# A layer norm's gain and offset: folded into the group's output, or applied to the whole block on GpSimd

## The reference

```
v = layernorm(gelu(v_raw), ln_w, ln_b)         # over the 1024 channels of a token
vc = v.reshape(b, 4, 128, 8, 128)              # chunk, token, group, channel
mixed = einsum('gts,bnsgc->bntgc', w_s, vc) + b_s[group, token]
y_b = gelu(u_raw) * mixed * silu(g_raw)
```

## Time and profile before

| | |
|---|---|
| time of three runs | 1870.9 us median (1867.78 to 1877.06) |
| the profiled execution | 1870.9 us, its span 1869.0 us |
| mean granted TensorE clock | 0.949 |
| busy: TensorE, VectorE, ScalarE, GpSimd | 90%, 43%, 33%, 28% |
| head phase, gate phase | about 49 to 490 us, about 490 to 670 us |

### The profile page before, as it was taken

How to read it: one execution, slowest core, us unless ns; L and a number is a source line. 1 busy time by engine, 2 the same in 40 slices (tenths; PEclk the granted TensorE clock), 3 DMA queues, 4 the chain that set the end, 5 groups by cost and what they waited for, 6 DMA issues and landing times.

```text
span 1869.0 us, 22809 instructions
## 1 busy us (share of the span) xinstructions
PE 1680.4 (90%) x9242; PEld 1301.9 (70%) x9242; DVE 801.9 (43%) x1246; ACT 625.8 (33%) x1008; POOL 531.5 (28%) x279
## 2 busy tenths in 40 slices
PE   4999989899899789998968998999996889999996
PEld 2888878799687667776737897555683665555564
DVE  2237377464674520111156611666413445444422
ACT  3421222212323222223232122666413223555632
POOL 2331222212122343334324222332423321010230
PEclk8999999899999889999989999999997889999998
DMA  4231322212323425443301221000010120000101
GB/s 136 91 125 36 100 68 67 74 38 67 90 81 88 125 76 171 135 135 112 102 23 46 68 75 45 18 18 18 23 57 26 30 65 20 15 18 24 46 23 46
DMA packets 128674, 122.46 MB, mean 66 GB/s; under 512 B 11237, under 2 KB 125041, under 8 KB 128593
## 3 DMA queue, kind: packets, MB, share of 16 engines
q1 hardware_dynamic: 128592, 121.33, 20.8%
HBM read 116.87 MB, written 2.10 MB: 64 GB/s over the span
## 4 chain that ended last, share of the span: by engine, by line
PE 64%; DVE 13%; issue 12%; POOL 7%; ACT 3%; DMA 1%; SPq 0%; DVEq 0%; POOLq 0%; ACTq 0%
PE ps L1771 6%; PE ps L1772 5%; PE ps L1773 5%; PE ps L1817 5%; POOL w_lo L987 4%; PE ps L2171 3%; PE ps L1971 3%; PE ps L2150 3%; PE ps L1972 3%; PE ps L1973 3%; PE ps L2160 3%; PE ps L1935 2%; PE ps L2037 2%; PE ps L2028 2%; PE ps L1845 2%
## 5 line engine op out<-in xcount | busy, mean ns | idle before, releaser
L987 POOL TENSOR_TENSOR w_lo<-raw,w_hi 128x2048 fp32r<-128x2048 f32 (+2 forms) x86 | 373.6, 4345 | 805.2 <-ACT w_hi L595 726.6
L1771 PE MATMUL ps<-h_hi,w_hi 128*128 128x512 f32 x656 | 276.2, 421 | 53.2 <-POOL h_lo L1040 14.5
L1772 PE MATMUL ps<-h_lo,w_hi 128*128 128x512 f32 x656 | 266.9, 407 | 0.0
L1773 PE MATMUL ps<-h_hi,w_lo 128*128 128x512 f32 x656 | 266.4, 406 | 0.0
L595 ACT ACTIVATE w_hi<-raw 128x2048 fp32r<-128x2048 f32 (+1 forms) x78 | 147.4, 1890 | 325.9 <-DMA raw<-in_w_in_dram 105.5
L1771 PEld LDWEIGHTS ps<-h_hi,w_hi 128*128 128x128 f32 x656 | 130.0, 198 | 95.3 <-issue 34.6
L1773 PEld LDWEIGHTS ps<-h_hi,w_lo 128*128 128x128 f32 x656 | 129.8, 198 | 29.3
L1772 PEld LDWEIGHTS ps<-h_lo,w_hi 128*128 128x128 f32 x656 | 130.6, 199 | 25.0 <-issue 0.2
L1817 PE MATMUL ps<-qf,kf 128*128 128x64 f32 x448 | 87.2, 276 | 7.1 <-DVE tot_b L1240 6.1
L944 ACT ACTIVATE pT_b<-ps 128x512 f32<-128x512 f32 x96 | 56.9, 594 | 94.2 <-PE ps L2160 93.0
L1817 PE MATMUL ps<-qb,kb 128*128 128x64 f32 x448 | 87.7, 278 | 0.0
(11 more groups left out here) (349 smaller groups left out, 3539.1 us busy)
## 6 DMA issues: line engine op xcount, KB each, us to landing
raw<-in_w_in_dram SPq DMA_DIRECT2D x32, 1024.0 KB
raw<-in_ada_w_dram SPq DMA_DIRECT2D x24, 1024.0 KB
raw<-in_a_w_in_dram SPq DMA_DIRECT2D x10, 1024.0 KB
raw<-in_w_in_dram SPq DMA_DIRECT2D x16, 512.0 KB
raw<-in_b_w_in_dram SPq DMA_DIRECT2D x5, 1024.0 KB
raw<-in_w_proj_a_dram SPq DMA_DIRECT2D x4, 1024.0 KB
raw<-in_w_proj_b_dram SPq DMA_DIRECT2D x4, 1024.0 KB
raw<-in_w_out_dram SPq DMA_DIRECT2D x4, 1024.0 KB
```

Of the source, the lines that this page charges most:

```text
L987: nc.gpsimd.tensor_tensor(w_lo[:, ph.w(s), c], raw[:, s % 2, c], w_hi[:, ph.w(s), c].bitcast(F32), ALU.subtract).then_inc(s_lo, 1)
L1771: mm(ps[:, j, :], wh[:, k, c], xh[:, k, :], start=(k == 0), stop=False)
L1772: mm(ps[:, j, :], wh[:, k, c], xl[:, k, :], start=False, stop=False)
L1773: last = mm(ps[:, j, :], wl[:, k, c], xh[:, k, :], start=False, stop=(k == KT - 1))
```

## The change

The gain and the offset are applied to `vs` itself. SP loads `ln_w` and `ln_b` as two broadcasts to all 128 partitions (512 KB each) behind the first iteration's strips, in place of two small rows in the setup. The statistics leave the head loop: `norm_v` in slot 0 of the gate phase takes them from the finished `vs`, in eight instructions of 512 elements, each followed by a wait, and scales the four chunks in the same slot. GpSimd then multiplies each chunk by the gain and adds the offset, eight passes of 128x1024 elements; `lo` of gate strip 2 stands after the fourth of them. The first mix waits for the last (`s_vs`). `weight_sums`, `ws_sum`, `ln_cols` and `offsets` go, and `combine` is a plain addition of the bias. `v_bn` shrinks and moves, so that the two broadcasts fit.

```diff
-        v_bn = at("v_bn", [P, NT, 6 * PAIRS], F32, r_yb + 8 * KB)
-        ws_sum = at("ws_sum", [P, GCH, P], F32, r_yb + 12 * KB)
+        ln_w_all = at("ln_w_all", [P, D], F32, r_yb + 8 * KB)
+        ln_b_all = at("ln_b_all", [P, D], F32, r_yb + 12 * KB)
...
-            for n, name in enumerate(("ln_w", "ln_b")):
-                sp.dma_start(ln_rows[n * GCH:(n + 1) * GCH, :], t[name].rearrange("a b -> (a b)").rearrange("(k p) -> k p", p=P)).then_inc(s_const, 16)
...
             heads_it(0)
+            sp.dma_start(ln_w_all[:, :], t["ln_w"].partition_broadcast(P)).then_inc(s_lnp, 16)
+            sp.dma_start(ln_b_all[:, :], t["ln_b"].partition_broadcast(P)).then_inc(s_lnp, 16)
...
             lo(gates, 0, 0)
-            lo(gates, 0, 2)
+            pool.wait_ge(s_lnp, 48)
+            for n in range(NT):
+                pool.wait_ge(s_ln, 3 + n)
+                nc.gpsimd.tensor_tensor(vs[:, n, :], vs[:, n, :], ln_w_all[:, :], ALU.mult).then_inc(s_pool, 1)
+                pool.wait_ge(s_pool, n + 1)
+                nc.gpsimd.tensor_tensor(vs[:, n, :], vs[:, n, :], ln_b_all[:, :], ALU.add).then_inc(s_vs, 1)
+                if n == 1:
+                    lo(gates, 0, 2)
...
-                            dve.wait_ge(s_free, heads.t(it, s) + j + 1)
-                            for n in range(2 * j, 2 * j + 2):
-                                v.bn_stats(v_bn[:, n, bass.ds(6 * it, 6)], vs[:, n, bass.ds(it * STRIP, STRIP)])
...
             def norm_v():
                 for n in range(NT):
-                    last = v.bn_aggr(v_stat[:, n, :], v_bn[:, n, :].rearrange("p (i c) -> p i c", c=6))
-                link(last)
+                    for h in range(2):
+                        link(v.bn_stats(v_bn[:, h, :], vs[:, n, h * S:(h + 1) * S]))
+                    link(v.bn_aggr(v_stat[:, n, :], v_bn[:, :, :]))
                 link(v.tensor_scalar(v_rstd[:, :], v_stat[:, :, 1], LN_EPS, None, ALU.add))
                 v.reciprocal(v_stat[:, :, 1], v_rstd[:, :]).then_inc(s_ln, 1)
-
-            def scale_v():
                 dve.wait_ge(s_ln, 2)
                 for n in range(NT):
                     v.tensor_scalar(vs[:, n, :], vs[:, n, :], v_stat[:, n, 0:1], v_rstd[:, n:n + 1],
-                                    ALU.subtract, ALU.mult).then_inc(s_vs, 1)
-
-            def offsets():
-                dve.wait_ge(s_lnp, 16)
-                dve.wait_ge(s_wsum, 2)
-                for g in range(GCH):
-                    last = v.scalar_tensor_tensor(bs_all[:, g, :], ws_sum[:, g, :], ln_cols[:, GCH + g:GCH + g + 1], bs_all[:, g, :],
-                                                  ALU.mult, ALU.add)
-                link(last)
-
+                                    ALU.subtract, ALU.mult).then_inc(s_ln, 1)
+
+            dve.wait_ge(s_lnp, 48)
...
-                link(v.scalar_tensor_tensor(tmp[:, 3, :].rearrange("p (n t) -> p n t", t=P), ps[:, 7, :].rearrange("p (n t) -> p n t", t=P),
-                                            ln_cols[:, g:g + 1], bs_all[:, g, :].unsqueeze(1).to_broadcast([P, NT, P]),
-                                            ALU.mult, ALU.add))
+                link(v.tensor_tensor(tmp[:, 3, :].rearrange("p (n t) -> p n t", t=P), ps[:, 7, :].rearrange("p (n t) -> p n t", t=P),
+                                     bs_all[:, g, :].unsqueeze(1).to_broadcast([P, NT, P]), ALU.add))
...
-            nc.tensor.transpose(ps[:, 3, P:P + 2 * GCH], ln_rows[0:2 * GCH, :], ident[0:2 * GCH, 0:2 * GCH])
...
-            def weight_sums():
-                pe.wait_ge(s_wst, 2)
-                for a in range(2):
-                    last = mm(ps[:, 4 + a, :], ones[:, :], wsT[:, 4 * a:4 * a + 4, :].rearrange("p g s -> p (g s)"), start=True, stop=True)
-                last.then_inc(s_wsum, 1)
```

More of the change, by code:

```diff
@@ L238, in block_kernel @@
         VROWS = rows
-        N_CONST = 16 * (4 + len(ROW))
+        N_CONST = 16 * (2 + len(ROW))
         def cols(name):
@@ L265, in block_kernel @@
         v_rstd = at("v_rstd", [P, NT], F32, r_mv + 32)
-        ln_rows = at("ln_rows", [P, P], F32, r_tmp + 512)
-        ln_cols = at("ln_cols", [P, 2 * GCH], F32, r_mv + 64)
+        v_bn = at("v_bn", [P, 2, 6], F32, r_mv + 64)
         sink8 = at("sink8", [P, A_HEADS], F32, region(64))
@@ L318, in block_kernel @@
         s_lnp = sem("s_lnp")
-        s_wsum = sem("s_wsum")
-        s_gain = sem("s_gain")
         s_mix = sem("s_mix")
@@ L630, in head_tiles @@
                     if kind == "ada":
[L631 to L634, removed]
                         ada_part(heads, it, s, 6 + heads.j(s))
@@ L1177, in _ @@
             link(v.tensor_copy(vec[:, 0:VROWS], ps[:, 3, 0:VROWS]))
-            link(v.tensor_copy(ln_cols[:, :], ps[:, 3, P:P + 2 * GCH]))
             link(v.tensor_copy(masks[:, :, :], masks_f[:, :, :]))
@@ L1383, in _ @@
                         norm_v()
-                    if tt == 1:
-                        scale_v()
                     if j == 0:
-                        if g == 1:
-                            offsets()
                         if g:
@@ L1855, in head_tiles @@
                         if first and s == 3:
-                            weight_sums()
                             pe.wait_ge(s_setup, 3)
```

## The result

The changed kernel takes 1889.6 us (median of five runs, 1886.45 to 1890.86) against 1869.3 us (median of five, 1867.78 to 1877.06). The ratio is 1.010, 95% interval 1.0077 to 1.0125. Forecast were 1889.3 us, and slower with a chance of 0.82. The profiled execution took 1891.4 us, its span 1889.5: 20.5 over the span of before. The two medians differ by 20.3 us and the prediction's sum was 18.4, so the terms are to be checked one by one.

The account below looks back on a forecast made before the run. In the edited stage VectorE and TensorE hand work to each other without slack, and GpSimd's lock holds VectorE. 21.6 - 1.05 - 1.7 - 0.4 = +18.4 on 1870.9 gives 1889.3 us, range 1876 to 1898.

Parts of the forecast that it names:

- Statistics and root: Gate phase slot 0: eight 512-element statistics at 0.69 us, 6.7 us in all against 0.61; square root on ScalarE at 506.3.
- The lock alternates: Gate phase slot 0: VectorE and GpSimd alternate, one operation each; TensorE's decay matmuls start 23.0 us later.
- the row at 244: VectorE's L1212, issued at 245.06 after GpSimd asked at 244.24, took 5.61 us; read as alternation rather than issue order.
- The clock: Decay matmuls to first mix: TensorE starts at 1.2 GHz for 3.5 us after the long pause, giving 1.4 us back.
- the stretch at 49.5: TensorE at 1.2 GHz for 3.5 us from 49.5 to 53, losing 1.8 us; model for the speed after the pause.
- The start: Setup: two small loads, one transpose and one copy go, -1.05 us; weight sums ahead of the ada matmuls go, -1.7.
- Broadcasts: 1 MB more ahead of the next iteration's weights fits into a transfer standstill: 0; 4.0 us without that cover.
- Offsets: The eight operations (2.17 us) go, but VectorE waited behind them for the mix anyway: 0.
- `combine`: Loses its scalar on VectorE, 0.75 to 0.69 us, eight times: -0.4.
- A: Gate phase slot 0: VectorE keeps the lock, or it hardly bites; not slower, 1879 or 1874 us; chance 0.15.
- B: Broadcasts delay the next weights (up to +4) or the clock stays low for 7 us (+3): 1892 to 1897; chance 0.10.
- C: Start gains remain and GpSimd is hidden, passes over before 524.6: about 1866 us; chance 0.03.

Follow-up runs that it names:

- e2: Changed kernel with GpSimd's passes writing to a spare buffer, the first mix waiting for the scaling only: stage +23.2 us, by the ratio +15.5 us over before.
- e3: Changed kernel with each chunk's two passes replaced by six memsets, the mix waiting for the last: stage +13.0 us, by the ratio +8.0 us over before.
- e7: Changed kernel with 104 extra matmuls filling TensorE's pause ahead of the decay matmuls: median 1882.16 us, by the ratio +10.3 us over before.
- e8: Kernel before with gain and offset left out altogether, statistics staying in the head loop: stage 0, by the ratio -5.0 us (-9.5 to -0.6).
- e1: Changed kernel without the eight GpSimd passes, statistics and scaling kept: stage +9.3 us, by the ratio +7.7 us over before.
- e4: Changed kernel with the four gain multiplications alone, offset passes left out: median 1884.22 us, stage +14.3 us, by the ratio +12.5 us over before.
- e11: Kernel before with the two rows loaded with the spatial weights and the weight sums made in the setup: by the ratio +1.3 us (-2.8 to +5.2).
- e9: Kernel before with GpSimd's weight subtraction held until VectorE's products are done: stage -5.0 us, by the ratio +0.6 us (-3.6 to +4.5).
- e5: Changed kernel with gain and offset passes on VectorE, GpSimd doing only its subtraction: median 1891.2 us, stage +19.5 us, by the ratio +17.4 us over before.

## Why the prediction was right

**Statistics and root, right.** Eight of 512 elements take 0.70 us apart (estimate 0.69); from their start to the scaling it is 503.28 - 495.84 = 7.44 us, 7.42 foreseen. (8 x 0.73 + 4 x 0.2 is 6.64 and not 6.7, too little to matter.)

**The lock alternates, right.** e2 and e3 settle that it is the contention: without reader the cost stays, and beside memsets the products take 0.69. The turns come as listed, down to the fourth pass that holds nobody. The chain from first product to decay matmuls is 39.98 us; 23.0 on top of 18.08 were 41.1. The 1.1 less are three small terms: GpSimd starts 0.96 us behind the first scaling and not 1.5; its nine operations last 26.4 us and not 27.3, so a handover is (26.4 - 23.7) / 9 = 0.3 us and not 0.4; and TensorE starts 0.3 us behind the last pass and not 0.05. What makes the turns alternate was not tried. The prediction read the row at 244 as speaking against issue order, but it doesn't: GpSimd's operation was issued first, at 244.24, and VectorE's at 245.06. In the changed kernel too, GpSimd's next pass is issued at 519.90 and VectorE's next product at 520.40. Serving whoever asked first gives the same turns here as strict alternation.

**The clock, wrong by 3.2 us, and outside its own bounds of -1.8 to +1.4.** I had TensorE back at full speed 3.5 us after a long pause, from the stretch at 49.5, and 1.4 us gained. It stayed low for 10.7 us, and from decay matmuls to mix it took 14.14 us: 1.8 lost against 12.38. e7 confirms the size with 9.16 at full clock. The step that failed is the reading of that row. The 3.5 us were only the end of a longer low stretch, as the stretch ahead of them in the kernel before shows:

```profile
36.00:49.50 13.50, 8.75 (x18) 5.19 (x18) 8.14 (x8) 5.60 (x9) 8.63 (x7) 0.50 0.24 78
```

The long pause there (7.03 us) had ended at 38.41, so behind it the clock stayed low for some 14.6 us, until 53, with TensorE at work but for three pauses of 0.8 to 0.9 us. Other pauses of the same trace gave other lengths: the clock was 0.50 for 5.5 us behind one of 6.62 (364.97 to 370.5), and for 3.6 us behind one of 5.89 (486.40 to 490.0).

**The start, right in size, in part by luck.** -2.75 foreseen (1.05 + 1.7), -3.09 at slot 0. The two terms are there: behind the setup's copies the lead is 0.94 us (13.49 for 14.43, VectorE's `masks`), and the weight sums gave their 1.7, from 2.04 at the `w_lo` ahead of them (72.24 for 74.28) to 3.77 at the transfer (79.83 for 83.60). But the lead then grew by things that the prediction didn't name. That transfer landed in 5.23 us, not 6.51, so its `w_lo` came 5.0 us earlier (87.08 for 92.12). A later one came 6.5 earlier (112.72 for 119.20), because the clock in between stayed at 1.00 where it had fallen. The stretch in the changed kernel:

```profile
92.50:96.00 3.50, 3.50 (x29) 3.50 (x30) 2.17 (x3) 0.05 (x1) 0.00 (x0) 1.00 0.91 301
```

The stretch of the same work in the kernel before:

```profile
97.50:101.00 3.50, 3.48 (x16) 3.50 (x17) 1.95 (x3) 0.00 (x0) 0.00 (x0) 0.51 0.95 314
```

In the second iteration the changed kernel then had a low stretch that before hadn't (272 to 279 was at 1.00 there), and about 3 us of the lead went back:

```profile
268.50:275.30 6.80, 6.80 (x34) 6.80 (x33) 4.80 (x9) 0.00 (x0) 0.00 (x0) 0.50 0.00 0
```

**The small terms.** Broadcasts, put at nothing: right. The next weight load was issued at 105.45 (111.98 before), 6.5 us earlier, and its `w_lo` came 6.5 earlier too, so nothing was lost in between. Offsets, put at nothing: right (e8). `combine`: I took 0.4 off for eight. It gives 0.1 in the first group (e8), but behind the first mix as a whole the difference moved by 0.1 us only (20.57 to 20.5).

Sum by what was measured, in the profiled runs: 23.7 for the stage less 3.1 for the start is 20.6, against 20.5 of span. Mine was 18.4: +3.2 (clock), -1.1 (chain), -0.3 (start), +0.4 (`combine`) leads from one to the other. The medians differ by 20.3 us, and the ratio says 18.7. The agreement of 1889.3 with 1889.6 is luck: the clock's error was partly made good by the chain's, and before's median is 1869.3 in these runs and not 1870.9. The mechanism, the waits and most of the cost are not luck.

**The rivals.** A failed: there was no burst. By e3 its price in the stage would have been about 9 us, an estimate, where the prediction had 8.5. B's broadcasts did nothing; its clock came true in part, with 10.7 us of low clock for the 7 it named. C had no part.

**Left open.** What sets how long the clock stays low: behind e1's pause of 9.62 us it took 14.74 to the mix, behind e4's of 16.0 it took 13.40, behind the changed kernel's 24.59 it took 14.14. Why e7's gain is some 4 us larger by the ratio than in its stage, and why e11's lead doesn't show in its median, was not tried further. Slot 0 begins between 487.7 and 497.8 in the runs that share the changed kernel's start, and between 494.1 and 500.4 in the two that share the start of before, e9 and before itself, so a lead of 3 us in one trace is less than what runs differ by. Whether the lock follows issue order or alternates by itself is open too.

## What to carry to other kernels

Before work is moved to GpSimd because it is idle there, look at what VectorE does in the same stretch: here a GpSimd operation that reads SBUF held up VectorE's operations with two SBUF inputs and its tensor_scalar, one for one, and left those with an input in PSUM alone. It did so even when nothing waited for the passes (e2), and each of the last four, 2.4 us long, cost the chain 2.15 us (e4). Folding a per-channel factor into an output that is evicted anyway cost 0.1 us or less there, and some 3 us of preparation at the start in the traces (0.6 to 9.5 by e8's ratio). Applying it to the whole block made the stage 14 us longer on GpSimd and some 10 on VectorE (e2 and e5, each less e1). And a pause of TensorE can cost more than its length: add what the low clock takes behind it, here 5.0 us (e7), and when that is read from a row, look where its low stretch begins. Look one group further before a local gain is booked (e9).

## What was unexpected about the hardware

- Under contention the two engines took turns: behind each GpSimd operation exactly one waiting VectorE operation came through, even where VectorE issued its next one 0.08 us before the end of the last (`qb`, `kb`: 2.82 us each behind passes of 2.78 and 2.67).
- Memsets on GpSimd left VectorE's products alone (0.69 us) but stretched tensor_scalar by half (4.41 for 2.97).
- The granted clock stayed at 0.50 for 10.7 us after a pause of 24.59 us, with TensorE busy throughout, where behind pauses of 6.62 and 5.89 us in the kernel before it had stayed low for 5.5 and 3.6 us.
